# A decoder step on one core: the sampled sequences' keys turned on VectorE, and their attention interleaved with the prompt's out-projection

## The chip, the core and the metric

The kernel runs on one core of one Trainium2 chip. The core has TensorE (PE, with its weight loads PEld), VectorE (DVE), ScalarE (ACT), GpSimd (POOL) and SyncE (SP, which issues most transfers); 16 DMA engines move the data. The metric is device time in microseconds (us), lower is better.

## What is computed

One inference step of a decoder layer: 1,024 prompt tokens and 8 sampled sequences of 8 new tokens each, whose 1,024 past keys and values lie in a paged cache (8 pages of 128 keys for each sequence). The part that matters here, cut from the reference:

```python
def sample_attn(q, k, v, lam, k_past, v_past, rel_bias):     # 8 sequences, 8 heads, 2 maps a head
    s_past = diff_logits(q, q_pos, k_past, jnp.arange(past), rel_bias)
    s_new = diff_logits(q, q_pos, k, q_pos, rel_bias)
    w = diff_weights(jnp.concatenate([s_past, s_new], axis=-1), lam)
    return einsum('bhqk,bkhe->bqhe', w[..., :past], v_past) + einsum(..., w[..., past:], v)
...
x = x + jnp.einsum('btd,de->bte', g_a * y_a + g_b * y_b, lp['w_out'])       # out-projection
h2 = rms_norm(x, lp['norm_ffn'])
up = jnp.einsum('btd,df->btf', h2, lp['w_up'])                              # then the channel mixer
```

`diff_weights` is softmax of map 0 minus lam times softmax of map 1. All of it is float32. Where a product is not done in plain f32, each operand is split into a high part (rounded to fp32r) and a low part (the rest), and three products are summed: high by high, high by low, low by high.

## The kernel before

The program has four stages, each a block that all five engines enter and leave together: `front` (norm), `heads` (input projection, RG-LRU and prompt attention, one head after another), `sampled_and_out` (L1406 on) and `mixer`. At the end of a block every engine waits for all others, SP too. The change is in `sampled_and_out` and in the last transfers that SP issues in `heads`.

**A sampled sequence, before.** Each engine has the same loop over turns b = 0 to 8, 8 heads in each. For a head, TensorE turns the 1,024 keys (`turn_keys`, 8 transposes of 128x128 at L1735 into two banks `tb`), ScalarE copies a bank out as the high part (L1879), VectorE subtracts for the low part (L2045), and TensorE multiplies both parts with the queries (L1776, `qd`, 6 products of 344 columns). After the heads, VectorE sums and finds the maximum (L2012, L2090), ScalarE takes the exponent (L1921). The weights are turned by products with `C`, which holds the softmax's divisor and the signs (L1752, L1757), and are multiplied with the values (`page`, L1722: 32 columns of weights by 512 columns of values, into one of four strips of 32 partitions). A last step turns the result (`fold_heads`, L1710). Softmax and values of sequence b-1 lie in turn b. SP loads keys a sequence ahead into `k_raw` (two buffers of 8 pages) and values into `v_raw` (8 pages), a page being 512 KB; each page's number is first read from the page table (L1621).

**The out-projection, before.** After the last turn `out_tile(t)` (L1807) multiplies 128 merged tokens with `w_out`: 8 row blocks by 2 halves by 3 products, 48 products of 512 columns; there are 9 tiles, the last with 64 tokens. Tile 0 and 1 are begun in the last turn. Between tiles, `turn` (L1821) transposes the normed rows of the tile before, and `first_unit` (L1831) is the first unit of the mixer.

**What sets the order.** Every engine runs its list in program order and waits on semaphores. SP's list is one queue: a page load that waits for `page_done` holds all behind it.

Of the kernel before, what the change touches and what calls it, by code (L numbers as in the profile page):

```python
# [7 lines left out]
F32 = mybir.dt.float32  # L8
F32R = mybir.dt.float32r
# [381 lines left out]
def heads(nc, sb, sem, ins, outs, c):  # L391
# [206 lines left out]
    with nc.Block() as block:  # L598
# [19 lines left out]
        def _(sp):  # L618
# [9 lines left out]

            def load_pages(i):

                for n in (2 * i, 2 * i + 1):
                    page = sp.value_load(c.ptab[0:1, n:n + 1], min_val=0, max_val=ins["cache_k"].shape[1] - 1)
                    sp.dma_start(c.k0[:, c.k_first[n], :], ins["cache_k"][0, bass.ds(page, 1), :, :, :]
                                 .rearrange("a p h n -> p (a h n)")).then_inc(c.k_in[0][n // 4], 16)
# [7 lines left out]
            def body(f, first, last):  # L642
                m = 0
                for s in (TURN0 if first else TURN):
# [12 lines left out]
                    if s[0] == "P" and s[2] == 2:  # L657
                        g, ahead = W_NEXT[s[1]]
                        sp.wait_ge(ring_done, cur(f, NRING, RING[s]))
                        sp.sem_inc(settled, 1)  # L660
                        if last and ahead:
                            load_pages(done_last.index(s))
                        else:
                            load_w(f + ahead, g)
# [24 lines left out]
                    if s == ("QK", 7) and not last:  # L689
                        sp.wait_ge(c.tiles_out, 16 * 3)  # L690
# [34 lines left out]
            def load_sampled_bias():  # L725

                by_map = c.sbias_dram.rearrange("o (h m t) n -> m (o h) t n", h=H, m=2)
                for m in range(2):
                    sp.dma_start(by_map[m], bass.AP(tensor=c.bias_rows_dram.tensor, offset=DEC_T - 1,
                                                    ap=[[NU, H], [-1, DEC_T], [1, NKEYS]])).then_inc(c.tiles_out, 16)  # L730
# [505 lines left out]
        def _(pe):  # L1236
# [138 lines left out]
            pe.wait_ge(ttr_done, 16 * (H + 1))  # L1375
            for hf in range(2):
                pe.wait_ge(c.k_in[0][hf], 64)
                for n in range(4 * hf, 4 * hf + 4):
                    last_ = pe.transpose(ps[:, 3 + hf, 128 * (n % 4):128 * (n % 4 + 1)],
                                         c.k0[:, c.k_first[n], 0:128], c.ident[:, :])  # L1380
                last_.then_inc(c.tk0_done, 1)

SC = NKEYS // 3


def pair_select():

    row = np.arange(128)  # L1390
    head, m, t = row // 16, row // 8 % 2, row % 8
# [5 lines left out]
PV_EARLY = {}  # L1397
PV_AT = {4: (0, 1, 2, 3), 5: (), 6: (), 7: (), 8: (4, 5, 6, NPAGES)}
LAST = DEC_B - 1
OUT_SPLITS = [("m", 0), ("w", 0), ("w", 1), ("w", 2), ("w", 3), ("m", 1), ("w", 4), ("w", 5), ("w", 6), ("w", 7)]  # L1400
OUT_AT = {5: [("m", 0)], 6: [("w", 0)], 7: [("w", 1)], 8: [("w", 2), ("w", 3)]}
OUT_LOW = [x for x in OUT_SPLITS if x[0] == "m" or x[1] >= 4]
POOL_LOW = [x for h in range(H + 1) for x in OUT_AT.get(h, ()) if x not in OUT_LOW]


def sampled_and_out(nc, sb, sem, ins, outs, c):  # L1406
# [3 lines left out]
    S3 = ps[:, 0:3, 0:SC]  # L1410
    tb = [ps[:, 3, :], ps[:, 4, :]]
    pt = ps[:, 5, :]
    o2 = ps[:, 6, :]
    ptn = ps[:, 7, 0:NS]

    v_raw = sb("v_raw", [128, NPAGES, D], F32, 32768)
    vn_raw = sb("vn_raw", [128, D], F32, 65536)
    k_raw = [c.k0, sb("k1", [128, NPAGES, D], F32, 108544)]
    qd = sb("qd", [128, H * 128], F32R, 141312)
    slo = sb("slo", [128, NKEYS], F32, 145408)  # L1420
    sbias = sb("sbias", [128, NKEYS], F32, 150528)
    P = sb("P", [128, NKEYS], F32, 154656)
    pt_sb = sb("pt_sb", [128, NPAGES + 1, NS], F32, 158784)
    o2s = sb("o2s", [128, 512], F32, 163392)
    oT = sb("s_oT", [128, H, NS], F32, 167488)
    mg = sb("s_mg", [128, H, NS], F32, 169536)
    sel = sb("sel", [128, NS + 1], F32, 171584)
    p_new = sb("p_new", [128, 2, NS], F32, 176640)
    zeros = sb("s_zeros", [128, 2, DEC_T], F32, 177152)
    C = sb("C", [128, NS], F32, 172160)  # L1430
    sgn = sb("sgn", [128, 2], F32, 172416)
    mx = sb("s_mx", [128, 4], F32, 172448)
    eps = c.eps
    kt = sb("kt", [128, 2, 2, NKEYS], F32R, 178048)
    kt_hi, kt_lo = kt[:, 0, :, :], kt[:, 1, :, :]
    kn = sb("kn", [128, 2, H, NS], F32R, 206848)
    xn = sb("o_xn", [128, 2, D], F32, 202752)
# [8 lines left out]
    def strips(part, at):  # L1446

        q = qd[part, :]
        return bass.AP(tensor=q.tensor, offset=q.offset + at, ap=[q.ap[0], [144, HH], [1, DEC_T]])

    def q_hi_of(part, m, h0):

        return strips(part, 144 * h0 + DEC_T * m)

    def q_lo_of(part, m, h0):

        return strips(part, 144 * h0 + DEC_T * m + (NS if h0 < HH else -NS))

    def half_rows(s):

        lo = slice(NS, 128) if s == 0 else slice(0, NS)
        hi = slice(0, NS) if s == 0 else slice(NS, 128)
        return hi, lo
# [7 lines left out]
    v_in = [sem(f"v_in{n}") for n in range(NPAGES)]  # L1471
    vn_in = sem("vn_in")
    s_fill = sem("s_fill")
    tk_done = sem("tk_done")
    kthi_done = sem("kthi_done")
# [1361 lines left out]
```

## Time and profile before

| | us |
|---|---|
| median of 2 runs | 2019.01 (2018.39 to 2019.62) |
| the profiled execution's own time | 2017.05 |
| its span | 2015.2 |
| TensorE busy in it | 1967.5 |
| VectorE busy | 1312.9 |
| ScalarE busy | 937.4 |
| GpSimd busy | 37.0 |

The page gives one profiled execution. The span is cut into 40 slices of 50 us; GB/s says what the DMA engines moved in each. In a row of the timeline stand start, duration, engine, line, operation, output and inputs, shape and count; in square brackets, how long the engine stood idle before and for whom. A matmul's duration includes its way through the array, so the step from one start to the next tells what it costs.

### The profile page before, as it was taken

The numbers are of one execution on the slowest core, as the hardware profiler recorded it, in microseconds if no ns is written. First come the engines' busy times: TensorE is split into PE (matmuls) and PEld (weight loads), VectorE is DVE, ScalarE is ACT, GpSimd is POOL, SyncE is SP. The second block draws the span as 40 slices with busy tenths as digits, with TensorE's granted clock in tenths as the row PEclk, the third lists the DMA queues.
The fourth block names the chain that finished last, engine by engine and source line by source line (L and its number), as shares of the span: only waits on it lengthen the run. The fifth ranks groups of instructions, "written<-read, shape, count | busy, mean of one in ns | idle before, by whom it ended". The sixth has DMA issues, their size and how long they took to land. (4 is left out here: it accounts for less than half of the span.)

```text
span 2015.2 us, 35806 instructions
## 1 busy us (share of the span) xinstructions
PE 1967.5 (98%) x11872; PEld 1801.8 (89%) x11872; DVE 1312.9 (65%) x2891; ACT 937.4 (47%) x1705; POOL 37.0 (2%) x126
## 2 busy tenths in 40 slices
PE   6999999999999999899999999999999999999998
PEld 6999999999999999767768798999999998989896
DVE  6767667676676767666644485666657574748476
ACT  5766665657575757555554241322223131314033
POOL 0000000000000000000020000000000000000000
PEclk9999999999999999999999999999999999999999
DMA  6411111111111112599973121111111120202012
GB/s 197 150 58 54 58 53 57 53 57 53 57 53 57 53 55 76 199 349 338 342 278 110 35 81 32 55 42 53 42 44 52 32 63 22 73 22 73 5 50 100
DMA packets 167452, 183.25 MB, mean 91 GB/s; under 512 B 11045, under 2 KB 139589, under 8 KB 167349
## 3 DMA queue, kind: packets, MB, share of 16 engines
q1 hardware_dynamic: 166137, 181.24, 27.3%
q8 instruction: 43, 0.70, 0.1%
q10 hardware_dynamic: 1212, 0.81, 0.1%
q14 instruction: 60, 0.49, 0.1%
HBM read 162.82 MB, written 24.46 MB: 93 GB/s over the span
## 5 line engine op out<-in xcount | busy, mean ns | idle before, releaser
L1250 PE MATMUL ps<-h_hi,w_hi 128*128 128x384 f32 (+1 forms) x1152 | 387.0, 336 | 5.1 <-DVEq L967 3.4
L1250 PE MATMUL ps<-h_hi,w_lo 128*128 128x384 f32 (+1 forms) x1152 | 376.8, 327 | 0.0
L1250 PE MATMUL ps<-h_lo,w_hi 128*128 128x384 f32 (+1 forms) x1152 | 376.8, 327 | 0.0
L2410 PE MATMUL ps<-h_hi,f_w_hi 128*128 128x320 f32 (+1 forms) x1136 | 370.7, 326 | 0.8 <-PEq L1563 0.8
L2410 PE MATMUL ps<-h_hi,f_w_lo 128*128 128x320 f32 (+1 forms) x1136 | 370.4, 326 | 0.0
L2410 PE MATMUL ps<-h_lo,f_w_hi 128*128 128x320 f32 (+1 forms) x1136 | 370.2, 326 | 0.0
L2489 ACT ACTIVATE yc<-ps,f_prm 128x384 f32<-128x384 f32 x144 | 93.5, 654 | 555.7 <-PE ps L2410 382.8
L2390 PE MATMUL ps<-d_hi,act 128*128 128x512 f32 x816 | 257.0, 390 | 0.5 <-issue 0.5
L1250 PEld LDWEIGHTS ps<-h_hi,w_hi 128*128 128x128 f32 x1152 | 217.3, 189 | 9.0 <-issue 4.0
L1250 PEld LDWEIGHTS ps<-h_lo,w_hi 128*128 128x128 f32 x1152 | 217.4, 189 | 0.6
L1250 PEld LDWEIGHTS ps<-h_hi,w_lo 128*128 128x128 f32 x1152 | 217.0, 188 | 0.0
L2410 PEld LDWEIGHTS ps<-h_hi,f_w_hi 128*128 128x128 f32 x1136 | 213.2, 188 | 1.5 <-issue 1.1
L2410 PEld LDWEIGHTS ps<-h_lo,f_w_hi 128*128 128x128 f32 x1136 | 213.2, 188 | 0.3
L2410 PEld LDWEIGHTS ps<-h_hi,f_w_lo 128*128 128x128 f32 x1136 | 213.2, 188 | 0.0
L2544 DVE TENSOR_TENSOR x<-x,ps 128x512 f32<-128x512 f32 x144 | 97.8, 686 | 139.6 <-PE ps L2390 137.7
L2390 PEld LDWEIGHTS ps<-d_hi,act 128*128 128x128 f32 x816 | 153.2, 188 | 32.8 <-issue 0.7
L2390 PE MATMUL ps<-d_lo,act 128*128 128x512 f32 x432 | 168.2, 389 | 0.0
L2615 DVE SCALAR_TENSOR_TENSOR yc<-ps,f_prm,yc 128x383 f32<-128x383 f32 x144 | 82.2, 571 | 85.8 <-ACT yc L2489 82.3
L2045 DVE TENSOR_TENSOR kt<-ps,kt 128x512 fp32r<-128x512 f32 x128 | 82.7, 686 | 58.7 <-ACT kt L1879 58.3
L927 ACT ACTIVATE E<-E,nmx 128x256 f32<-128x256 f32 (+7 forms) x128 | 98.1, 768 | 14.3 <-DVE nmx L1195 9.8
L1191 DVE CUSTOM_DVE_ANT_0 E<-ps,bias 128x256 f32<-128x256 f32 (+7 forms) x128 | 91.4, 751 | 18.6 <-PE ps L1338 18.0
L1879 ACT ACTIVATE kt<-ps 128x512 fp32r<-128x512 f32 x128 | 72.1, 595 | 63.0 <-PE ps L1735 59.8
(301 smaller groups left out, 3181.0 us busy)
## 6 DMA issues: line engine op xcount, KB each, us to landing
k<-in_cache_k SPq DMA_DIRECT2D x64, 512.0 KB, 5.8
v_raw<-in_cache_v SPq DMA_DIRECT2D x64, 512.0 KB, 6.2
w_raw<-in_w_in SPq DMA_DIRECT2D x48, 512.0 KB, 4.0
f_raw<-in_w_up SPq DMA_DIRECT2D x48, 512.0 KB, 3.9
f_raw<-in_w_down SPq DMA_DIRECT2D x24, 512.0 KB, 3.5
bias<-bias_tiles_dram SPq DMA_DIRECT2D x8, 576.0 KB, 3.7
merged_dram<-mg SPq DMA_DIRECT2D x8, 544.0 KB, 2.7
ow_raw<-in_w_out SPq DMA_DIRECT2D x8, 512.0 KB, 7.5
```

Source lines behind the costliest of these rows:

```text
L927: act.activation(E[i][:, 0:n], E[i][:, 0:n], ACT.Exp, bias=nmx[:, i:i + 1], accum_out=den[:, i:i + 1]).then_inc(exp_done, 1)
L1191: dve.tensor_tensor_reduce(out=halves(E[i], j), in0=scores(i, j, first), in1=halves(bias, j, c0), scale=1.0, scalar=-3e38, op0=ALU.add, op ...
L1250: last_ = pe.matmul(bank(s)[:, 0:n], w[:, W_SLOT[g], k, :], x[:, k, off:off + n], start=(k == 0 and i == 0), stop=(k == KT - 1 and i == 2))
L1879: act.activation(kt_hi[:, h % 2, 512 * hf:512 * (hf + 1)], tb[hf], ACT.Copy)\
L2045: dve.tensor_tensor(kt_lo[:, h % 2, at], tb[hf], kt_hi[:, h % 2, at].bitcast(F32), ALU.subtract).then_inc(ktlo_done, 1)
L2390: l_ = pe.matmul(ps[:, down_bank(e), :], a, w[:, j, 512 * hf:512 * (hf + 1)], start=(j == 0 and i == 0), stop=(j == GF - 1 and i == len(pa ...
L2410: l_ = pe.matmul(ps[:, e % 6, 0:n], w[:, p, k, :], x[:, k, off:off + n], start=(k == 0 and i == 0), stop=(k == KT - 1 and i == 2))
L2489: act.activation(yc[:, e % 3, 0:n], ps[:, e % 6, 0:n], ACT.Identity, bias=prm[:, p, FCONV_W:FCONV_W + 1], scale=prm[:, p, FCONV_W - 1:FCON ...
L2544: dve.tensor_tensor(x2, x2, ps[:, down_bank(e), :], ALU.add).then_inc(add_done, 1)
L2615: link(dve.scalar_tensor_tensor(out=y[:, 1:np_], in0=x[:, 0:np_ - 1], scalar=w[1], in1=y[:, 1:np_], op0=ALU.mult, op1=ALU.add))
```

## The change

The diff is long; what it does, part by part:

- **Scores.** Keys are no longer turned on TensorE. VectorE transposes each page in place, 32x32 block by block (L1981 of the changed kernel, `STREAM_TRANSPOSE`, 8 a sequence). Scores are plain f32 products of 32 partitions by 32 columns of queries with 256 columns of keys (L1664, 128 a sequence), laid so that 16 consecutive ones lie at 16 different places of the array (4 groups of partitions `i`, 4 strips of outputs `h`), each group of partitions with a PSUM bank of its own. Splitting into high and low, its sums and the copies out fall away; the bias is added from PSUM (five operations instead of two sums and one).
- **Out-projection.** Tiles 0 to 6 go into the turns: step b of `sampled` does tile b-1 in five pieces (`fill`, 16+8+8+8+8 products) between scores, weights and values. Tiles 7 and 8 remain at the end. `w_out` is loaded and split at the stage's start. The low part of a tile is formed by GpSimd.
- **Values** have 4 page buffers instead of 8 (`vr`, `NV = 4`). Their loads stand ahead of the keys of two sequences later, each waiting for the buffer's `page_done`.
- **SP in `heads`.** Behind the last head's store of `merged_dram`, SP now loads 4 pages of keys and 4 of values, before the block ends. Four more key pages stand ahead of it.
- **Order.** Loops are unrolled, norms use Ln and Exp instead of Sqrt, and tiles are placed elsewhere in SBUF.

```diff
-                        for cc in range(3):
-                            keys = slice(SC * cc, SC * (cc + 1))
-                            for x, k in enumerate((kt_hi, kt_lo)):
-                                last = pe.matmul(S3[:, cc, :], qd[:, 128 * g:128 * (g + 1)], k[:, g % 2, keys],
-                                                 start=(g % HH == 0 and x == 0), stop=(g % HH == HH - 1 and x == 1))
...
+                for e in range(2):
+                    for j in range(NQ):
+                        for h in range(HH):
+                            J = NQ * (HH * e + h) + j
+                            for i in range(NQ):
+                                part = slice(32 * i, 32 * i + 32)
+                                pe.matmul(S[32 * h:32 * h + 32, i, :], qd[part, J, :],
+                                          keys[part, :, 32 * J:32 * J + 32],
+                                          start=(e == 0 and j == 0), stop=(e == 1 and j == NQ - 1))
...
+            for b in range(DEC_B):
+                t = b - 1
+                scores(b)
+                if b > 0:
+                    fill(t, 0)
+                    fold_heads(b - 1)
+                turn_weights(b)
+                if b > 0:
+                    fill(t, 1)
+                for run in range(4):
+                    values(b, run)
+                    if b > 0 and run < 3:
+                        fill(t, run + 2)
...
+                if b > 0:
+                    load_m(b)
+                    if b < LAST:
+                        load_x(b)
+                load_values(b, (4, 5))
+                load_values(b, (6, 7))
+                load_values(b + 1, (0, 1))
+                load_keys(b + 2, range(0, 4))
+                load_values(b + 1, (2, 3))
+                load_keys(b + 2, range(4, 8))
...
+                add_half(t - 1, 1)
+                turn_keys(b + 1, (0, 1))
+                softmax(b)
+                turn_keys(b + 1, (2,))
+                weights(b)
+                fold_rows(b - 1)
+                turn_keys(b + 1, (3, 4))
+                add_half(t, 0)
+                turn_keys(b + 1, (5, 6, 7))
...
+                        if last:
+                            load_next_keys(range(4, NPAGES))
+                            load_values()
```

**TensorE, first turn of the sampled stage.** Of the kernel before, two heads of sequence 0; `kt` holds the turned keys, `qd` the queries:

```order
L1703 UNCONDITIONAL_BRANCH [waits barrier_Pool_Activation_PE_DVE_SP_release]
L1735 MATMUL ps<-ident,k 128x128 [waits tk0_done,ktlo_done]
L1735 MATMUL ps<-ident,k 128x128 x3
L1735 MATMUL ps<-ident,k 128x128 [waits ktlo_done]
L1735 MATMUL ps<-ident,k 128x128 x3
L1776 MATMUL ps<-kt,qd 128x344 [waits ktn_done,ktlo_done,qdlo_done]
L1776 MATMUL ps<-kt,qd 128x344 x5
L1735 MATMUL ps<-ident,k 128x128 [waits ktlo_done]
```

Of the changed kernel, from the scores of sequence 1 on (`m_hi` and `w_hi` are a tile of the out-projection):

```order
L1664 MATMUL ps<-k,qd 32x256 [waits s_ttr_done,kt_done,qd_done]
L1664 MATMUL ps<-k,qd 32x256 x127
L1671 MATMUL ps<-k_new,qn 32x8 [waits ptc_done]
L1671 MATMUL ps<-k_new,qn 32x8 x7
L1739 MATMUL ps<-w_hi,m_hi 128x512 [waits ow_dlo_done,o_mplo_done]
...
L1712 MATMUL ps<-ident,o2s 128x128 [waits o2_done]
L1712 MATMUL ps<-ident,o2s 128x128 x3
L1682 MATMUL ps<-C,P 128x64 [waits ptc_done,c_done]
```

The transposes and their exchange with ScalarE and VectorE in every head are gone; one wait for all turned pages (`kt_done`) stands ahead of 128 score products, and out-projection products lie between them and the wait for the softmax (`c_done`).

**SP, end of `heads`.** Before, the store of the last head's merged rows is the last transfer of the block:

```order
L675 DMA out_v_rows_prompt<-rows 128x2x128 [waits row_done]
L678 DMA out_v_rows_sample<-rows 64x128
L697 DMA merged_dram<-mg 128x1088 [waits mg_done]
L598 UNCONDITIONAL_BRANCH [waits rows_out1,rows_out0,st_out]
L1616 UNCONDITIONAL_BRANCH [waits barrier_Pool_Activation_PE_DVE_SP_release]
```

Now eight page loads lie between the store and the block's end; the last of the keys and the last of the values:

```order
L631 TENSOR_LOAD ptab
L631 ISA x2
L632 ISA
L632 DMA k<-in_cache_k 128x1024
...
L632 DMA vr<-in_cache_v 128x1024
L598 UNCONDITIONAL_BRANCH [waits rows_out1,rows_out0,st_out]
L1578 UNCONDITIONAL_BRANCH [waits barrier_Pool_Activation_PE_DVE_SP_release]
```

So what SP issues there now stands ahead of the barrier for all engines.

## Rows read from the trace of the kernel before

**Rows 1.** The page: busy time and share of the engines; GB/s in 40 slices.
```profile
PE 1967.5 (98%) x11872; PEld 1801.8 (89%) x11872; DVE 1312.9 (65%) x2891; ACT 937.4 (47%) x1705; POOL 37.0 (2%) x126
GB/s 197 150 58 54 58 53 57 53 57 53 57 53 57 53 55 76 199 349 338 342 278 110 35 81 32 55 42 53 42 44 52 32 63 22 73 22 73 5 50 100
```

**Rows 2.** Windows: stretch, its length, busy of each engine, PE's clock, DMA share, GB/s.
```profile
833.00:840.00 7.00, 3.87 (x16) 3.15 (x15) 4.50 (x11) 3.59 (x9) 1.48 (x5) 0.52 0.57 207
885.00:1010.00 125.00, 120.86 (x864) 89.61 (x864) 77.66 (x152) 72.81 (x139) 9.62 (x50) 1.00 0.90 341
1050.00:1142.00 92.00, 91.34 (x431) 73.59 (x430) 40.57 (x51) 33.44 (x53) 0.00 (x0) 1.00 0.24 72
```

**Rows 3.** Timeline of TensorE, one turn of the sampled stage.
```profile
963.02 2.00 PE L1752 MATMUL ps<-C,P 128*128 128x64 f32 x16
...
965.05 1.19 PE L1776 MATMUL ps<-kt,qd 128*128 128x344 f32 x6
...
967.99 1.93 PE L1722 MATMUL ps<-v_raw,pt_sb 128*32 128x512 f32 x16
969.84 1.09 PE L1735 MATMUL ps<-ident,k 128*128 128x128 f32 x8
...
978.39 1.95 PE L1722 MATMUL ps<-v_raw,pt_sb 128*32 128x512 f32 x16
...
981.10 1.09 PE L1735 MATMUL ps<-ident,k 128*128 128x128 f32 x8
...
985.22 0.60 PE L1710 MATMUL ps<-ident,o2s 128*128 128x128 f32 x4
...
987.69 0.55 PE L1752 MATMUL ps<-C,P 128*128 128x64 f32 x3
```

**Rows 4.** Timeline of TensorE at the out-projection; 48 products of one tile lie between.
```profile
1060.14 1.02 PE L1844 MATMUL ps<-P,ones 128*128 128x512 f32 x2
1061.00 1.04 PE L1821 MATMUL ps<-ident,o_xn 128*128 128x128 f32 x8
...
1061.83 0.50 PE L1807 MATMUL ps<-ow_hi,m_hi 128*128 128x512 f32 x1
...
1072.87 1.04 PE L1821 MATMUL ps<-ident,o_xn 128*128 128x128 f32 x8
```

**Rows 5.** Timeline of TensorE in `heads`, two products of 64 partitions at once.
```profile
813.30 0.40 PE L1338 MATMUL ps<-k_lo,q_hi 64*128 64x512 f32 x2
813.54 0.39 PE L1338 MATMUL ps<-k_hi,q_lo 64*128 64x512 f32 x2
```

**Rows 6.** By shape: busy us, mean ns of one; idle before it.
```profile
L2103 DVE TENSOR_TENSOR m_lo<-o_raw,m_hi 128x1024 fp32r<-128x1024 f32 x6 | 7.3, 1219 | 2.6 <-ACT m_hi L1948 2.6
L1191 DVE CUSTOM_DVE_ANT_0 E<-ps,bias 128x256 f32<-128x256 f32 x16 | 6.1, 415 | 0.0
L1921 ACT ACTIVATE P<-P,s_mx 128x1032 f32<-128x1032 f32 x8 | 9.3, 1158 | 3.2 <-DVE s_mx L2093 3.0
L1597 POOL TENSOR_TENSOR ow_lo<-ow_raw,ow_hi 128x1024 fp32r<-128x1024 f32 x4 | 10.5, 2638 | 0.5 <-ACT ow_hi L1895 0.5
```

**Rows 7.** DMA in 885 to 1010 us: busy tenths and GB/s in 40 slices of 3.1 us.
```profile
DMA  9999993899999928999999399999983999999758
GB/s 337 375 402 414 406 408 136 279 333 396 384 409 414 405 102 298 273 393 414 414 406 408 80 315 376 358 409 419 408 350 94 287 376 418 413 408 404 295 159 266
```

**Rows 8.** The page's DMA issues: count, KB each, median us to landing.
```profile
f_raw<-in_w_down SPq DMA_DIRECT2D x24, 512.0 KB, 3.5
```

**Rows 9.** Timeline of SP's queue at the end of `heads`.
```profile
833.70 0.36 SPq L697 DMA_DIRECT2D merged_dram<-mg  x1
835.94 2.57 SPq L1625 DMA_DIRECT2D k<-in_cache_k  x3
```

**Rows 10.** Timeline of TensorE: end of `heads`, begin of the mixer.
```profile
830.44 0.70 PE L1370 MATMUL ps<-sq,ones 128*128 128x256 f32 x2 [0.75 <-ACT oT L947]
...
1155.61 0.38 PE L2410 MATMUL ps<-h_hi,f_w_hi 128*128 128x320 f32 x1 [0.80 <-PEq L1563]
```

More of the change, by code:

```diff
@@ L1396 @@
 HH = H // 2
-PV_EARLY = {}
-PV_AT = {4: (0, 1, 2, 3), 5: (), 6: (), 7: (), 8: (4, 5, 6, NPAGES)}
+NQ = 4
+NV = 4
 LAST = DEC_B - 1
[L1400 to L1403, printed above, removed]
+NIN = 7
+KS = (4, 5, 6, 7, 0, 1, 2, 3)
@@ L1444, in strip, with quarter @@
         return o2[32 * q:32 * q + 32, :]
[L1446 to L1463, printed above, removed]
+    def quarter(x, i):
+        return x[:, 0:PAST].rearrange("p (n i c) -> p i n c", n=NPAGES, i=NQ)[:, i]
     def own_rows(hf):
@@ new lines, in values, with fold_heads, products, weights_wait @@
+                    if n < NPAGES:
+                        last.then_inc(page_done, 1)
+            def fold_heads(b):
+                pe.wait_ge(o2_done, b + 1)
+                for g in range(HH):
+                    last = pe.transpose(o2[:, 128 * g:128 * (g + 1)], o2s[b][:, 128 * g:128 * (g + 1)], c.ident[:, :])
+                last.then_inc(ot_done, 1)
+            def products(k):
+                return ((m_hi, w_hi(k)), (m_hi, w_lo(k)), (m_lo, w_hi(k)))
+            def weights_wait(k):
+                if k in POOL_W:
+                    pe.wait_ge(wplo_done, POOL_W.index(k) + 1)
+                else:
+                    pe.wait_ge(wdlo_done, DVE_W.index(k) + 1)
@@ new lines, in fill @@
+            def fill(t, part):
+                for at in range(*FILL[part]):
+                    hf, x = divmod(at, HALF)
+                    k, i = KS[x // 3], x % 3
+                    if x == 0:
+                        if hf == 0:
+                            pe.wait_ge(mplo_done, t + 1)
+                        if t > 0 or hf > 0:
+                            pe.wait_ge(add_done, 2 * t + hf)
+                    if t == 0 and hf == 0 and i == 0:
+                        weights_wait(k)
+                    m, w = products(k)[i]
+                    last = pe.matmul(part_sum, m[:, k, :], w[:, 512 * hf:512 * (hf + 1)],
+                                     start=(x == 0), stop=(x == HALF - 1))
+                    if x == HALF - 1:
+                        last.then_inc(half_done, 1)
@@ new lines, in out_tile @@
+            def out_tile(t, ks):
+                n, at = rows_of(t), bank_of(t)
+                if ks[0] == KS[0]:
+                    pe.wait_ge(mdlo_done, t - NIN + 1)
+                for k in ks:
+                    for hf in range(2):
+                        for i, (m, w) in enumerate(products(k)):
+                            last = pe.matmul(ps[0:n, at + hf, :], m[:, k, 0:n], w[:, 512 * hf:512 * (hf + 1)],
+                                             start=(k == KS[0] and i == 0), stop=(k == KS[-1] and i == 2))
+                if ks[-1] == KS[-1]:
@@ new lines, in _ @@
+            turn_keys(0, c.k_first)
+            signs()
+            turn_keys(1, (0, 1, 2))
+            softmax(0)
+            turn_keys(1, (3,))
+            weights(0)
+            turn_keys(1, (4, 5, 6, 7))
+            for k in DVE_W:
+                weight_low(k)
+            for b in range(1, DEC_B):
+                t = b - 1
+                if b > 1:
+                    add_half(t - 1, 1)
[7 more added lines that the diff above has]
+                turn_keys(b + 1, (5, 6, 7))
```

992 lines of the change are left out of this document (440 added, 552 removed).

## The prediction

> **What bounds the kernel now.** I read the busy shares first: TensorE is busy 98% of the span, no other engine over 65% [rows 1]. So time is won only where TensorE does less or waits less. The slices say where else to look: GB/s is near 340 in five slices of 40 and low elsewhere [rows 1], which is the sampled stage. The window of it has TensorE busy 120.86 of 125 us, VectorE 77.66, and 341 GB/s [rows 2]: TensorE bounds it, and the transfers are not far behind. The windows of the out-projection show TensorE full and only 72 GB/s [rows 2]. The change lays the two over each other, and takes work from TensorE.
>
> A turn's length is the step between two equal places: L1752 starts at 963.02, values at 967.99 take 1.85 (to 969.84) and at 978.39 another 2.71 (to 981.10), the turned weights 2.03 (to 965.05), the fold 0.60 [rows 3]. The next turn's L1752 starts at 987.69 [rows 3]: 24.7 us a turn (its 16 pages of 512 KB, 8.39 MB, at 341 GB/s give 24.6 [rows 2]). Turning keys and scoring take what is left, 24.7 - 4.6 - 2.0 - 0.6 = 17.5 us. The stretch that the change touches goes from the end of `heads` (831.1) to the first mixer product at 1155.6 [rows 10], 324.5 us.
>
> **The price of the new scores (S).** A plain f32 product of 512 columns takes 0.86 us (1060.14 to 1061.00, two instructions [rows 4]), so one of 256 columns 0.43, and 128 of them one behind another 55 us. But the eight value products of a run, the same kind with 32 columns of weights in four strips, take 1.85 us for 6.9 [rows 3]: 3.7 at once. And two products of 64 partitions in different groups of partitions take one step of 0.24 us [rows 5], as one product of the out-projection does (11.04 / 48 = 0.23 [rows 4]). No row shows both splits together. If all 16 places work at once, S is 3.4 us; if eight (four strips by the two groups that rows show), 6.9; if only the four strips overlap, 13.8. I take 5, between the first two, since each split alone runs at full rate. The Trainium skill (TensorE: Matmul & The Clock Gate, Part 3: Packing small matmuls) reports 10.6 times for 16 such places; by that S would be 55 / 10.6 = 5.2, an estimate that no run here shows yet.
>
> **A step of the changed stage on TensorE.** Out-projection tile 11.0 [rows 4], values 4.6, weights 2.0, fold 0.6 [rows 3], S 5, new keys 0.3, some restarts 0.4: 23.9 us, out of which a whole out-projection tile comes nearly free: before it was 24.7 and 11.0 apart.
>
> **What it waits for.** Per step the transfers are 16 pages, a merged tile and an `x` tile, 18 x 0.524 = 9.44 MB. The slices reach 402 to 419 GB/s while pages queue, and 279 to 376 in those behind a pause [rows 7]. At 405 a page is 1.29 us and a step 23.3; the four value buffers add pauses: values 4 and 5 are asked for only when 0 and 1 are used up, 2.7 + 1.8 us before they are wanted, and an unqueued 512 KB lands 3.5 us after issue [rows 8], two of them with SP's 1.1 us a page 4.6. Walked through from the end of values 4 and 5 of the step before: 14 transfers (2 values, 4 keys, 2 values, 4 keys, tile, `x`) run from 1.5 to 19.6; values 0 and 1 are used up at 17.6, so the next pair moves from 19.6 to 22.2 and is seen some 1 us later, at 23.2; it is wanted at 17.6 + 4.5 = 22.1. That is 1.1 us late, and I add 0.4 for the slower rate behind a pause: 23.9 + 1.5 = 25.4 us for steps 2 to 5. Steps 6 and 7 load no keys: 24. The Trainium skill (DMA: Bandwidth & Descriptors, Specifications) gives some 358 GB/s of HBM for a core: by it a step is 26.4 us of transfers and the sum 5 us more. The rows with 402 to 419 GB/s speak against it as a ceiling.
>
> VectorE has per step 8 transposes, the five bias and maximum operations (415 ns for 256 columns [rows 6]) 2.4 with what follows, 1.4 of residual, 0.9 of small ones. A 128x1024 transpose is in no row. The two shapes differ by 804 ns for 768 columns [rows 6], so 1024 columns without any start cost are 1.07 us, my lower bound; the upper is twice 1219 ns, as if each block were first filled and then emptied. I take 1.22, the nearest row: 9.8 + 4.7 = 14.5 us, hidden under TensorE's 24; without that cover it would be all of it. Its pages 0 to 2 stand ahead of the softmax, and the chain from scores over maximum (2.4), exponent (1158 ns [rows 6]) and divisor (0.5) takes 4.2, against 4.2 of cover by `fill` 0 and the fold. GpSimd's low part takes 2.6 [rows 6] in the 5 us of the scores.
>
> **The start.** All engines wait for SP at the block's end. Before, its last transfer was issued at 833.70 and the next stage's at 835.94 [rows 9]. Three pages took 2.57 us including the last's own time, 1.1 a page [rows 9]. Eight behind the store, 9 us, and four ahead of it that hold it back by about 1: the stage begins at 844.4 instead of some 834.5 (after the store, before the first load), ten microseconds in which TensorE does nothing. Then sequence 0 has no cover: 8 transposes 9.8, scores on a slow clock (PE's clock was 0.52 in 833 to 840 after a pause [rows 2]; 7), three more transposes beside, softmax 2.4, exponent 1.3, divisor 0.6, weights 2 to 4, values with two waits of 4.6 each for pages 4 to 7: 36 us in sum, for 12 us of TensorE's work. Sequence 1 waits for keys of sequence 2, asked for at the end of values 4 and 5: 27 us.
>
> **The end.** After the last values, tiles 7 and 8 (22), nine turns (9 x 0.83 = 7.5 [rows 4]), fold and sum 1.6, the mixer's first unit 8.5, waits 2.4: 42 us.
>
> **Sum.** 844.4 + 36 + 27 + 4 x 25.4 + 2 x 24 + 42 = 1099.0, where it was 1155.6: 56.6 us less. Checked by work: 8 x (17.5 - 5.3) = 98 us of TensorE saved, some 32 idle added at the start, some 9 in the steps. The profiled execution's own time is 2017.05, 1.8 over its span; the median is 2.0 above that. 2019.0 - 56.6 = 1962. A difference of 2% (40 us, below 1978.6) is about what a measurement can tell here.
>
> **The rivals.**
> - *Only the four strips overlap* (S = 13.8): the value rows show four at once and no more [rows 3]. Start +9, sequence 1 +6, four steps at 32.7 +29, two +17: 61 us back, 2024, slower than before. From S = 13 on the gain is gone. Against it: groups of partitions do overlap [rows 5]. 6 in 100.
> - *TensorE's clock drops*: steps with pauses of 1 to 2 us and small products run at 0.5 as at 833 to 840 [rows 2]; 7 x 20 us more, about 2100. Against it: the clock is 1.00 over 885 to 1010 with pauses in it [rows 2]. 3 in 100.
> - *The DMA engines bound every step* at the 341 GB/s of the window instead of 405: 27.7 + 1 us, 1978. For it: 279 to 376 GB/s behind each pause [rows 7]. Against: those are the pauses' own. 12 in 100.
> - *The transposes take 2.4 us*: the start grows by 13, each step to 27.5 since three stand in the softmax's chain; 1990. The Trainium skill (Vector Engine (DVE) Microarchitecture Reference, 3.8) says that a transpose sustains one element a cycle and lane, which speaks against this. 8 in 100.
> - *Better than that*: S at 3.4, pairs of values on time, the start 8 us shorter: 1940. 11 in 100.
>
> **Chances.** My forecast's own case, 1948 to 1976, has 60 in 100. The range 1938 to 1988 leaves out the two slow rivals, half of the transposes' and a third of the better case: it holds some 83 in 100. Faster by over 2%: the forecast's case, the better one and half of the DMA one, 0.76; slower by over 2% is the clock and a bad form of the strips, 0.04; the rest 0.20.
>
> **What the profile will show.** S: the step from L1664's first start to L1671's, 4 to 7 us. Steps of 24 to 27 us between two equal rows of L1682. The stage's first operation at about 844. VectorE's `STREAM_TRANSPOSE` at 1.1 to 1.3 us. Waits of L1703 for `vr` below 2 us a step and 3 to 5 in sequence 0. A clock below 1 only in sequence 0. The first mixer product near 1099. I am wrong if S is over 10, if a transpose takes over 2 us, or if the waits for pages exceed 4 us a step.

## The result and the profile after

The changed kernel takes 2002.0 us (median of 2 runs, 2001.8 to 2002.2) against 2019.0: a ratio of 0.992, interval 0.991 to 0.994. It is faster by 0.8%, 17 us, where the forecast said 57 us. The profiled execution's span is 2000.0 us, 15 under that of before.

From the page of the changed kernel: busy time of the engines, the GB/s, VectorE's transposes, the queue that brings instructions, and the page loads with their median time to landing.

```profile
PE 1910.3 (96%) x13152; PEld 1726.6 (86%) x13152; DVE 1280.0 (64%) x2835; ACT 877.6 (44%) x1694; POOL 37.5 (2%) x68
...
GB/s 201 150 59 55 58 54 57 54 57 54 57 54 57 54 55 76 207 279 291 304 312 233 58 64 21 66 32 54 43 54 43 40 56 23 73 22 74 9 46 101
...
q8 instruction: 55, 0.90, 0.2%
...
L1981 DVE STREAM_TRANSPOSE k<-k 128x1024 f32<-128x1024 f32 x64 | 75.2, 1218 | 46.2 <-DMA k<-in_cache_k 34.8
...
k<-in_cache_k SPq DMA_DIRECT2D x64, 512.0 KB, 6.2
vr<-in_cache_v SPq DMA_DIRECT2D x64, 512.0 KB, 5.0
```

Against [rows 1], TensorE is busy 57 us less, in 1,280 matmul rows more, and is at 96% of the span in place of 98%. The forecast had 98 us of its work off. Half-rate stretches count as busy, so part of that is hidden in the 57; the rest, and why only 17 us of time came of it, is what the experiments are about. The slices that had 338 to 349 GB/s have 279 to 312.

Windows of three steps (scores to scores) and three short ones, behind the holes that are told of below; columns as in [rows 2]:

```profile
915.00:947.00 32.00, 28.06 (x402) 17.61 (x411) 13.28 (x26) 8.47 (x27) 2.97 (x4) 0.95 0.85 307
979.00:1008.00 29.00, 25.97 (x381) 16.13 (x376) 13.28 (x26) 8.07 (x27) 2.40 (x4) 1.00 0.87 323
1040.00:1070.00 30.00, 26.58 (x414) 16.35 (x411) 13.28 (x26) 13.25 (x39) 3.49 (x4) 1.00 0.97 346
954.30:957.80 3.50, 3.50 (x63) 2.13 (x63) 0.99 (x5) 0.96 (x4) 0.00 (x0) 0.51 1.02 417
986.20:989.70 3.50, 3.50 (x66) 2.48 (x36) 2.07 (x13) 2.05 (x9) 0.00 (x0) 1.00 1.04 419
1015.80:1022.60 6.80, 6.80 (x33) 4.87 (x31) 3.50 (x15) 5.30 (x18) 0.19 (x1) 0.50 1.04 403
```

Before, 125 us of this stage had 121 of TensorE at clock 1.00 [rows 2]. Now a step of 32 us has 28 of it, and the clock is 0.51 in a stretch of 3.5 us in the next. Such a stretch follows five of the seven holes of sequences 1 to 7, of 3.4 us each, and of 6.8 us behind that of sequence 5 (1015.8). It does not follow that of sequence 4 (986.2), nor that of 6, and the steps that begin with these (979, 1040) are 29 to 30 us.

The timeline of TensorE over one step, from the scores of sequence 3 (L1664) to those of sequence 4; the 48 products of the tile (L1739) and most values (L1703) are left out. An x212 counts matmuls, each with a weight load of its own; a burst of scores has 256 of them, two to a product of the program:

```profile
946.72 4.55 PE L1664 MATMUL ps<-k,qd 32*32 32x256 f32 x212
954.25 2.15 PE L1664 MATMUL ps<-k,qd 32*32 32x256 f32 x44 [2.98 <-issue]
956.34 0.40 PE L1671 MATMUL ps<-k_new,qn 128*32 128x8 f32 x16
...
961.42 1.90 PE L1682 MATMUL ps<-C,P 128*128 128x64 f32 x16
...
973.63 1.05 PE L1703 MATMUL ps<-vr,pt_sb 128*32 128x512 f32 x4 [1.09 <-DMA vr<-in_cache_v]
...
978.51 1.34 PE L1664 MATMUL ps<-k,qd 32*32 32x256 f32 x56
```

The scores do not take 5 us but 9.6, from 946.72 to 956.34. The rate is as forecast: 212 in 4.55 us are 5.5 us for all 256, ten to eleven times as fast as the 55 us of one behind another. But 44 of them wait behind a hole of 2.98 us that no semaphore ends ("issue": the profile sees nothing that the engine waits for). In the waits of 830 to 1180 us (total, times, longest):

```profile
PE ps L1664 <- issue: 22.1, 8, 3.3
...
PE ps L1703 <- DMA vr<-in_cache_v: 7.0, 9, 2.8
```

Eight such holes, one in each burst, 22.1 us. (A bracket counts from the end of the matmul before, so from start to start a hole costs some 0.35 us more than it says.) Before, PE had no row that ends in "issue" in this stretch. Values wait 7.0 us for pages in all.

The start, in the timelines of SyncE's queue, of VectorE, and the end, in that of TensorE:

```profile
831.86 0.79 SPq L713 DMA_DIRECT2D merged_dram<-mg  x1
833.47 4.67 SPq L632 DMA_DIRECT2D k<-in_cache_k  x4
838.90 3.60 SPq L632 DMA_DIRECT2D vr<-in_cache_v  x4
843.03 0.33 SPq L1614 DMA_DIRECT2D sbias<-sbias_dram  x1
```

```profile
843.08 3.50 DVE L1981 STREAM_TRANSPOSE k<-k 128x1024 f32<-128x1024 f32 x3 [11.36 <-PEq L598]
```

```profile
1140.40 0.38 PE L2379 MATMUL ps<-h_hi,f_w_hi 128*128 128x320 f32 x1 [0.81 <-PEq L1541]
```

The first mixer product stands at 1140.4, 15.2 us earlier than in [rows 10], and 41.4 later than the forecast's 1099.0.

### The profile page after: what moved, and what is told of

The parts are those of the page before. It is cut to its first block and busy times, and to the rows that moved or that the text cites. A ratio compares the mean times of both kernels' runs of the same rounds, so it can differ in the third digit from the quotient of the medians.

```text
span 2000.0 us, 37541 instructions
## 1 busy us (share of the span) xinstructions
PE 1910.3 (96%) x13152; PEld 1726.6 (86%) x13152; DVE 1280.0 (64%) x2835; ACT 877.6 (44%) x1694; POOL 37.5 (2%) x68
## 5 line engine op out<-in xcount | busy, mean ns | idle before, releaser
L1981 DVE STREAM_TRANSPOSE k<-k 128x1024 f32<-128x1024 f32 x64 | 75.2, 1218 | 46.2 <-DMA k<-in_cache_k 34.8
L2359 PEld LDWEIGHTS ps<-d_lo,act 128*128 128x128 f32 x432 | 81.1, 188 | 16.6
```

What stands on the lines that cost most here:

```text
L1981: dve.transpose(keys, keys).then_inc(kt_done, 1)
L2359: l_ = pe.matmul(ps[:, down_bank(e), :], a, w[:, j, 512 * hf:512 * (hf + 1)], start=(j == 0 and i == 0), stop=(j == GF - 1 and i == len(pa ...
```

## Experiments: what the hole is

**Sixteen tiny products ahead of the stage.**

```diff
+            for _ in range(16):
+                pe.matmul(part_sum[:, 0:8], c.ident[:, :], c.ones[:, 0:8], start=True, stop=True)
             for b in range(DEC_B):
                 t = b - 1
                 scores(b)
```

> 16 tiny products (8 columns of ones into the bank that the tile's halves use later) stand ahead of sequence 0's scores; nothing else is changed. In the changed kernel each burst of 256 score products has one hole of about 3.3 us, at product 147, 204, 208, 212, 216, 220, 224 and 228 of the eight bursts. Theory A, the engine waits there for its next block of instructions: the blocks' borders lie at fixed distances in the instruction stream, so 64 more instructions ahead move every hole some 32 products earlier (about 115, 172, 176, ...) and leave its length at about 3.3 us; the total stays within 2 us of the changed kernel's. Theory B, the hole belongs to a place in the scores (a row of the array, a bank, data that comes late): the holes stay at 147, 204, 208, ...

Sequence 3 on TensorE's timeline:

```profile
947.57 3.92 PE L1664 MATMUL ps<-k,qd 32*32 32x256 f32 x180
955.23 3.27 PE L1664 MATMUL ps<-k,qd 32*32 32x256 f32 x76 [3.73 <-issue]
```

The hole has moved from matmul 212 to 180, by 32 (the 16 products are 32 matmuls), and in the others of sequences 1 to 6 from 204 ... 224 to 172 ... 192. The total is 2000.3 us in one run. So the place is one in the instruction stream, not in the scores. A step has some 380 matmuls, and in its 31.8 us the queue q8 moves three packets of 16 KB: one to about 127 matmuls with their weight loads, which I call a block. Theory B falls. In the first burst the hole came one block later, at 243. There the tiny products had run from 843.8 on, while the scores still waited for keys, and q8 moved a packet at 847.4, 5.7 us ahead of the scores at 853.1; in the changed kernel q8's first packet of the stage starts at 856.9, when the scores have run since 852.4. So the block with the border at 115 had been asked for early enough.

**Half the key columns.**

```diff
-     pe.matmul(S[32 * h:32 * h + 32, i, :], qd[part, J, :], keys[part, :, 32 * J:32 * J + 32],
+     pe.matmul(S[32 * h:32 * h + 32, i, 0:128], qd[part, J, :], keys[part, 0:4, 32 * J:32 * J + 32],
```

> Scores with half of the keys left out: each score product streams 128 columns in place of 256, with the same count of products. Theory A, a burst is set by the issue of its 512 instructions at about 21 ns a product: 256 x 21 = 5.4 us of work stay, the hole stays at 3.3 us or grows by nothing, and the burst keeps its 7 to 9.5 us. Theory B, the array (16 products side by side, columns streamed) sets it: the work falls from 5.4 to about 2.7 us and the burst to 6 us or below. Total by A within 5 us of the changed kernel's, by B 20 us lower.

```profile
945.09 3.05 PE L1664 MATMUL ps<-k,qd 32*32 32x128 f32 x212
952.50 1.35 PE L1664 MATMUL ps<-k,qd 32*32 32x128 f32 x44 [4.37 <-issue]
```

Neither theory held whole. The 212 now take 3.05 us instead of 4.55, so a burst is not bound by issue at 21 ns as I had said: columns count, though half of them save only a third. But the 1.4 us come back in the hole, 4.37 in place of 2.98, and the total hardly moves (1997.9 in one run). That is how a fixed delay behaves: the faster the block before is used up, the longer the wait for the next.

**Thin pages.**

```diff
-     sp.dma_start(dst, pool[0, bass.ds(page, 1), :, :, :].rearrange("a p h n -> p (a h n)"))
+     sp.dma_start(dst[:, 0:256], pool[0, bass.ds(page, 1), :, 0:2, :].rearrange("a p h n -> p (a h n)"))
```

> The page loads that the sampled stage issues bring 256 of 1,024 columns; three quarters of their data are left out, all instructions are the same. If transfers set the step (9.44 MB, 24 to 27 us at 1.22 to 1.29 us a page), it falls to what TensorE needs; so: theory A, TensorE's stream (work plus the instruction hole) sets 29 to 31 us a step, and a step loses only the 1 to 2 us that values now wait for a page: total 1990 to 1998. Theory B, transfers set it: steps fall to 24 to 26 us, total 1960 to 1970.

```profile
933.57 4.55 PE L1664 MATMUL ps<-k,qd 32*32 32x256 f32 x212
939.26 1.32 PE L1664 MATMUL ps<-k,qd 32*32 32x256 f32 x44 [1.14 <-issue]
```

```profile
934.00:960.00 26.00, 24.86 (x376) 15.73 (x348) 13.28 (x26) 8.12 (x26) 2.28 (x4) 1.00 0.39 122
```

1964.6 us in one run, Theory B's number, but not by its mechanism. With transfers at 0.39 the hole has shrunk to 1.14 us on sequence 3 and to 0.3 to 0.8 on the others from 1 on, there the clock never falls, no value waits, and steps are 25.4 to 26.4 us with TensorE busy 24.9 of 26. Without what its hole costs from start to start (0.7 to 1.5 us) each of these steps is 24.9 us: that is the stream's own work. My Theory A had the hole as independent of traffic, and that was wrong. TensorE enters the block ahead of the hole 128 matmuls before it. From there to the start of the next packet on q8 it is 3.5 us in the changed kernel and 0.8 here; to the scores' going on 5.9 and 3.6 (medians over sequences 1 to 6).

**Full pages, but few in flight during the scores.**

```diff
             def load_keys(b, pages):
                 if b < DEC_B:
-                    sp.wait_ge(score_done, b - 1)
+                    sp.wait_ge(score_done, b)
```

> SyncE issues the page loads of the keys two sequences ahead only behind the scores of the next sequence, one burst later than in the changed kernel; the same pages are loaded in full, but few are in flight while a burst of scores runs. In the changed kernel the border before the one with the hole is crossed at 948.3, the block's transfer starts 3.6 us later, takes 1.0, and the scores go on 5.9 us after the border; with thin pages that was 0.8 us, 1.3 and 3.5, and the hole 1.0 in place of 3.3. Theory A, the block of instructions stands behind page packets in the DMA engines: the transfer starts within 1 us of the border, the scores go on 3.5 us behind it, and the hole is 0.7 to 1.5 us, with full pages. Theory B, the lead has to do with something else that the thin pages changed: hole 3 us. Theory C for the time: pages then come late, steps of 31 to 35 us, total 2000 to 2030.

TensorE on sequence 3, the window of its burst, and q8 (packets, MB, share of 16 engines) from 1.2 to 2.4 us behind the entry into the block at 959.7:

```profile
958.11 4.56 PE L1664 MATMUL ps<-k,qd 32*32 32x256 f32 x212
963.31 1.32 PE L1664 MATMUL ps<-k,qd 32*32 32x256 f32 x44 [0.65 <-issue]
```

```profile
958.10:964.60 6.50, 5.85 (x262) 3.89 (x262) 0.00 (x0) 0.60 (x1) 1.97 (x2) 1.00 0.06 25
```

```profile
q8 instruction: 1, 0.02, 4.8%
```

The transfers stand at 0.06 to 0.24 in the bursts of sequences 1 to 6, where the changed kernel has 0.95 to 1.00. The hole is 0.65 us on sequence 3 and 0.1 to 0.4 on the other five, the packet starts 0.6 to 1.3 us after the border, and the burst takes 5.7 to 6.5 us, with full pages. (On sequence 7 pages are in flight again, 0.54 in the burst: the hole is 1.54.) In the changed kernel, which enters the block at 948.3, the packet starts at 951.9; its window, 3.5 to 4.9 us behind the entry:

```profile
q8 instruction: 1, 0.02, 4.4%
```

So Theory A is shown: TensorE's instructions come in blocks that the profile counts on the same 16 DMA engines as the pages, and while pages queue there a block's packet starts some 3 us later; the packet itself takes no longer (0.9 to 1.1 us on sequences 1 to 6, and 0.9 to 1.3 with few pages). In theory C only the size was off: 2046 us in one run, since everything that was held back comes late (steps of 38 us).

The Trainium skill (Runtime: NRT & Kernel Launch, Instruction fetch mechanics) says that each engine's instructions are refilled in 16 KiB blocks of 256 through a DMA queue of its own, and that this is mostly hidden. The trace agrees on the blocks (0.90 MB in 55 packets), and on their being hidden where instructions are slow; for the densest 5 us of this kernel it does not hold.

## Experiments: what the hole costs

**Slow work between the halves of the scores.** The last run of values of a sequence (`values(b, 3)`) is moved into the next sequence's scores.

```diff
-                scores(b)
+                scores(b, (0, 1))
+                if b > 0:
+                    values(b - 1, 3)
+                scores(b, (2, 3))
...
-                for run in range(4):
+                for run in range(3):
```

> The last run of values of a sequence (pages 6 and 7 and the new values, 6 products, 1.9 us) stands between the two halves of the next sequence's scores in place of ahead of them; same products, same data. Theory A, the hole in the scores is a late block of instructions, because 256 dense instructions are used up in 2.7 us while a block is asked for some 5.9 us before it can be used: 1.9 us of slower products in the block shorten the hole by about 1.8 us in each of seven bursts, total 13 us lower than the changed kernel's, 1985 to 1995. Theory B, the hole has another cause (a place in the scores): it keeps 3.3 us, total within 3 us, or higher by two changes of shape a step (1 to 2 us in all).

```profile
941.66 2.76 PE L1666 MATMUL ps<-k,qd 32*32 32x256 f32 x128
...
946.20 2.03 PE L1666 MATMUL ps<-k,qd 32*32 32x256 f32 x84
950.27 1.76 PE L1666 MATMUL ps<-k,qd 32*32 32x256 f32 x44 [2.05 <-issue]
```

1987.6 us, ratio to before 0.985 (0.983 to 0.987), some 14 us less than the changed kernel, as expected. The row shows 2.05 us; sequences 1 to 6 have 0.4 to 2.1 and sequence 7 none. So the 1.9 us of values did not come off each hole alike, but off the seven together: 8.1 us in place of 19.4.

**And eight products of the tile beside it.** Each later piece of the tile moves one place forward, and on VectorE `add_half(t, 0)` stands right behind `weights(b)`.

```diff
-FILL = ((0, 16), (16, 24), (24, 32), (32, 40), (40, 48))
+FILL = ((0, 8), (8, 24), (24, 32), (32, 40), (40, 48))
...
                 if b > 0:
                     values(b - 1, 3)
+                if b > 1:
+                    fill(t, 0)
                 scores(b, (2, 3))
```

> As the kernel with the last run of values between the halves of the scores, and behind that run stand the first 8 products of the next tile's half as well (1.8 us; every later piece of the tile moves one place forward, no product is added or left out; VectorE adds the first half to x right behind the weights' scale). The block of instructions with the scores then lasts 2.7 + 1.9 + 1.9 = 6.5 us against a lead of 5.9 to 7. Theory A: the hole (1.4 to 2.4 us with the values alone) falls to 0 to 0.5, steps fall from 29 to 27, total 1987.6 - 6 x 1.8 = 1975 to 1981. Rival, transfers: a step's page packets take 26.5 us of 16 engines and stand idle 3 to 4 us while SyncE waits for page buffers: steps stay at 28.5 to 30, total 1984 to 1989.

The hole was gone from sequence 2 on, and nothing was gained: 1987.1 us. TensorE on sequence 3, and VectorE ahead of its softmax:

```profile
940.64 2.76 PE L1666 MATMUL ps<-k,qd 32*32 32x256 f32 x128
...
947.23 2.76 PE L1666 MATMUL ps<-k,qd 32*32 32x256 f32 x128
...
956.95 2.14 PE L1686 MATMUL ps<-C,P 128*128 128x64 f32 x16 [2.37 <-DVE C L2024]
```

```profile
950.87 2.37 DVE L1993 STREAM_TRANSPOSE k<-k 128x1024 f32<-128x1024 f32 x2 [12.05 <-DMA k<-in_cache_k]
953.16 0.38 DVE L2009 CUSTOM_DVE_ANT_1 P<-ps,sbias 128x256 f32<-128x256 f32 x1
```

The scores are done at 950.2, but VectorE's order has two key pages ahead of the softmax. It had waited 12.05 us for them, began to turn them at 950.87, and reached the maxima at 953.16, 2.9 us late. TensorE's 2.37 us wait for the divisor is that delay. Whether the transfers' rate or VectorE's order made that wait, the next run decides.

**The softmax first on VectorE.**

```diff
                 softmax(b)
-                turn_keys(b + 1, (2,))
                 weights(b)
+                add_half(t, 0)
                 fold_rows(b - 1)
-                turn_keys(b + 1, (3, 4))
-                add_half(t, 0)
-                turn_keys(b + 1, (5, 6, 7))
+                turn_keys(b + 1, range(NPAGES))
```

(`turn_keys(b + 1, (0, 1))` ahead of `softmax(b)` is gone too; `add_half` stood there already in the kernel before this.)

> As the kernel with values and 8 tile products between the halves of the scores (1987.1 us), but VectorE runs the softmax and the weights' scale of a sequence first and turns all eight pages of the next sequence's keys behind them, in place of two ahead and one between. In that kernel VectorE stood 12.1 us waiting for a key page ahead of the softmax, which began 2.9 us after its scores, and TensorE waited 2.4 us for the weights' scale (9.9 us over five steps). Theory A, the wait moved from the hole to this place only by VectorE's order: it goes, steps fall from 29 to 27, total 1976 to 1982, and the 3 to 4 us of idle transfers stay. Theory B, the transfers bound the step: the keys then are turned too late, the next scores wait for them, and the steps stay at 28.5 to 29.5, total 1984 to 1989.

```profile
912.00:1017.60 105.60, 103.90 (x1514) 63.88 (x1512) 51.89 (x104) 33.50 (x104) 11.36 (x13) 1.00 0.99 361
```

```profile
962.75 1.05 PE L1707 MATMUL ps<-vr,pt_sb 128*32 128x512 f32 x4 [0.35 <-DMA vr<-in_cache_v]
963.98 1.05 PE L1707 MATMUL ps<-vr,pt_sb 128*32 128x512 f32 x4 [0.18 <-DMA vr<-in_cache_v]
```

1977.1 us, ratio 0.980 (0.978 to 0.981): 10 us less, Theory A. The window is that of steps 2 to 5: 26.4 us each, TensorE busy in 26.0, the clock 1.00 and the transfers at 0.99, 361 GB/s. The busy time flatters the stream: added up from start to start its products are 24.9 us, as with thin pages, and the other 1.5 us of a step stand at the values of pages 4 and 5, which wait for their pages; the two rows are one such place. So once the hole is gone the late values are what is left of the waits, and the 16 engines are busy all the time. No run tells apart how much of it is the transfers' rate and how much the order of the loads. In one point Theory A was wrong: the idle time of the transfers went as well. They are asked for when TensorE and VectorE have used up pages, and both do so earlier.

## Experiments: transfers, cover and the barrier

**Two key pages ahead of the value loads**, once in the changed kernel as it was and once with the spread scores.

```diff
+                load_keys(b + 2, (0, 1))
                 load_values(b, (4, 5))
                 load_values(b, (6, 7))
                 load_values(b + 1, (0, 1))
-                load_keys(b + 2, range(0, 4))
+                load_keys(b + 2, (2, 3))
```

> The changed kernel with its scores in one burst as they were, and only the two key pages loaded ahead of the loads that wait for a values buffer. Theory A, the hole and the half clock behind it set the step, and transfers only through the 1 us for which values wait: total 1995 to 2002. Theory B, the engines' idle 3.5 us a step is what the step lacks: 1980 to 1990.

> As the kernel before, and two of the eight key pages of a sequence are loaded ahead of the first load that waits for a values buffer, so that the 16 engines have 2.6 us of packets in the 3.5 us in which they stood idle. If the transfers bound the step once the hole is gone: 1 to 2.6 us less a step, total 5 to 15 lower than the kernel before (1965 to 1975). If TensorE bounds it (25.7 us of work a step): within 3 us of it. Against it: values of pages 4 to 7 may land later and their products wait: up to 10 us more.

With the scores in one burst: 2002.2 us (0.990 to 0.994 of before), nothing gained; the holes are as long. With them spread: 1979.7 (0.980 to 0.983), 7 us less, in the span (5 to 15) that I had given to transfers as what bounds the step. The rows say otherwise.

```profile
937.00:964.00 27.00, 26.31 (x381) 15.98 (x380) 13.00 (x27) 8.37 (x26) 2.62 (x4) 1.00 0.97 350
992.00:1019.00 27.00, 26.15 (x402) 16.13 (x406) 13.23 (x26) 8.38 (x26) 2.91 (x5) 1.00 0.98 351
```

```profile
PE ps L1708 <- DMA vr<-in_cache_v: 5.0, 11, 1.0
...
DVE k L1994 <- DMA k<-in_cache_k: 0.7, 3, 0.3
```

Steps are 26.7 us with the transfers at 0.97 to 0.98, and VectorE waits 0.7 us for keys over five steps, where it had waited 12.05 in one. So the transfers did not set the changed kernel's step. The 7 us are those of the wait on VectorE, taken away from the other side: by earlier keys here, by its order in the run before.

**Without the tile.** All but the first and last product of each half are left out.

```diff
                     m, w = products(k)[i]
+                    if 0 < x < HALF - 1:
+                        continue
                     last = pe.matmul(part_sum, m[:, k, :], w[:, 512 * hf:512 * (hf + 1)],
```

> Of each half of the out-projection's tile only the first and the last product are left, 44 of 48 products of a step are left out, so that a step's floor without the tile shows. Worked out: 11 to 12 us of TensorE go. Theory A, TensorE's stream sets the changed kernel's step (31 us): the step becomes 31 - 12 = 19 by TensorE and is then caught by the transfers at 25 to 27 us; total 2002 - 7 x 4 to 7 x 6 = 1960 to 1975. Theory B, something that is not TensorE (turning of keys on VectorE, softmax, the new K and V) sets the step: it stays at 29 us or above, total over 1990.

```profile
962.24 3.68 PE L1682 MATMUL ps<-C,P 128*128 128x64 f32 x16 [3.19 <-DVE C L2014]
...
973.44 1.05 PE L1703 MATMUL ps<-vr,pt_sb 128*32 128x512 f32 x4 [1.77 <-DMA vr<-in_cache_v]
975.46 1.92 PE L1703 MATMUL ps<-vr,pt_sb 128*32 128x512 f32 x4 [0.96 <-DMA vr<-in_cache_v]
```

```profile
948.00:982.00 34.00, 24.76 (x365) 11.68 (x366) 13.18 (x26) 8.59 (x27) 2.94 (x5) 0.70 0.81 285
```

2009.6 us in one run, beside 2000.3 for the kernel with the sixteen tiny products on the same chip: slower, with 12 us less of products a step. My Theory A subtracted work where it had to follow waits. What the tile had covered is bare: 3.19 us for the divisor, 1.77 and 0.96 for values. And the clock is 0.70 over the step, so that the weights take 3.68 us instead of 1.90. Not one limit but a chain of waits, run through at half clock for much of the step, keeps it at 31 to 34 us; which share each has was not measured.

**The barrier.** The eight page loads behind the last head's store are issued at the sampled stage's start instead.

```diff
                         if last:
-                            load_next_keys(range(4, NPAGES))
-                            load_values()
...
             sp.dma_start(sel[:, :], ins["pair_select"]).then_inc(const_in, 16)
+            for n in range(4, NPAGES):
+                load(1, n, ins["cache_k"], c.k1[:, n, :], c.k_in[1][n // 2])
+            for n in range(NV):
+                load(0, n, ins["cache_v"], vr[:, n, :], c.v_in[n])
```

> The 8 page loads behind the last head's store (4 of keys, 4 of values) are issued at the start of the sampled stage, behind its two small constants, so that the barrier no longer stands behind them on SyncE. My theory (the barrier waits for SyncE, which is held by its loads: the last head's work ended at 829.1, the stage's first instructions stand at 843.1): the stage starts 7 to 9 us earlier and the total falls by 5 to 9 us. Rival: the loads are only moved behind and sequence 0's and 1's values and keys come that much later, total within 2 us.

> Both edits of the two kernels before, in one kernel. If they act at different places (the stage's start; each of seven steps), the gains add: 1985 to 1995 less 5 to 9, so 1978 to 1988 by my theories; by the rivals, 2000 or more.

```profile
846.89 5.05 PE L1665 MATMUL ps<-k,qd 32*32 32x256 f32 x147 [17.29 <-DVE k L1982]
...
881.87 2.53 PE L1665 MATMUL ps<-k,qd 32*32 32x256 f32 x114
```

The first scores stand at 846.9 instead of 852.4, 5.5 us earlier, those of sequence 1 at 881.9 instead of 883.8: 2.0. The total is 2000.9 (0.991 to 0.994), not told apart from the changed kernel's. With the values between the scores 1986.7, again no more than 1 us. Here the rival was right: the pages that were moved behind come later.

**All of them.** The kernel with spread scores and keys ahead, plus the barrier edit; and that with the softmax first.

> As the kernel with spread scores and two key pages loaded ahead (1979.7 us), and with the 8 page loads behind the barrier. On its own that edit moved the start 5.5 us and the total 1.1 us. If the transfers of the first two sequences bound their start: again 0 to 2 us lower, 1977 to 1980. If TensorE does: 4 to 6 us lower, 1974 to 1976.

> As the kernel before this, with VectorE's softmax first. Its keys come early enough, so no wait stands ahead of the softmax there: by Theory A within 2 us of the kernel before (the wait that the order would take away is not there), and by a rival, turning that no longer fills VectorE's pause for the exponential ends later and the next scores wait: up to 5 us more.

1975.3 us (ratio 0.978 to 0.980) and 1974.6 (0.978 to 0.981). The barrier edit brought 4.4 us here (the two intervals just touch), near the lower end of what I gave for a start bound by TensorE, and the order of VectorE nothing measurable more, as Theory A said. The first mixer product of the last one:

```profile
1111.54 0.38 PE L2390 MATMUL ps<-h_hi,f_w_hi 128*128 128x320 f32 x1 [0.81 <-PEq L1538]
```

## Why the forecast was wrong

The steps of the sum, in its own terms, against the changed kernel's trace:

| term | forecast | measured | off |
|---|---|---|---|
| stage begins | 844.4 | 843.1 | -1.3 |
| sequence 0 | 36 | 40.7 (843.1 to 883.8) | +4.7 |
| sequence 1 | 27 | 31.2 (to 915.0) | +4.2 |
| steps 2 to 5 | 4 x 25.4 | 125.5 (to 1040.5) | +23.9 |
| steps 6 and 7 | 2 x 24 | 59.2 (to 1099.7) | +11.2 |
| the end | 42 | 40.7 (to 1140.4) | -1.3 |

They sum to the 41.4 us of the first mixer product.

- **S, the price of the scores, was right, and the step that failed is the one that put it into the step as 5 us of time.** With the hole it is 8.6 to 9.6 us in steps 2 to 5. The array's work is 5.4 to 5.5 us, where the forecast had 5 and the Trainium skill's 10.6 times (TensorE: Matmul & The Clock Gate, Part 3) gave 5.2; the trace agrees with both. The profile's sign for S, "4 to 7 us from L1664's first start to L1671's", failed: it is 7.3 to 9.7. I priced 256 matmuls by the array alone and did not ask how they come to the engine. Every stretch of before was thinner: 16 matmuls in the 1.93 us of values, 0.12 us each [rows 3], one in 0.23 us in the out-projection [rows 4]. At some 20 ns each, no row of before stood near.
- **The rival "TensorE's clock drops" had 3 in 100, and it half came**: the clock is 0.50 for 3.4 or 6.8 us behind most holes. Over steps 2 to 5 the clock lost 1.5 us a step, where the rival had 20. The evidence against it, a full clock in 885 to 1010, had 4.1 us of pauses in five turns [rows 2]; now one pause is of 3.
- **The term 23.9 for TensorE's stream was 1 us too small** without any hole: 24.9, from start to start. A piece of 8 tile products takes 2.05 us instead of 1.84 (11.0 for 48 [rows 4]), the 16 of the first 3.83, the tile 12.0 for 11.0. S is 5.4 for 5, the values are 4.8 for 4.6; weights, fold and new keys are 2.6 for 2.9. I had given 0.4 for restarts; each piece of the tile costs 0.15 to 0.2 us over its share of 11.0, and a step has five.
- **The late values were right**: 1.5 us forecast, 1.8 a step as the mean of steps 2 to 5 from start to start (the brackets of the waits have 0.8 of it, 1.09 in the row at 973.63). So were the transposes (1.22 us against 1.218), the start behind the barrier and the end. Sequence 0 had a hole too, of 2.65 us.
- **So the step of 25.4** (steps 2 to 5 are 31.4 in the trace) is 24.9 of work at full clock, 3.2 of hole (12.6 us in four, 11.2 of them in the brackets), 1.5 of clock and 1.8 of late values, each from start to start. The hole with the clock behind it is 4.7 of the 6.0 us missed, the stream 1.0 and the values 0.3.
- **That the DMA engines bound each step** (12 in 100, at 1978) was not so in the changed kernel, whose steps 2 to 5 have them at 0.79 to 0.87, yet they made the hole. With the hole out they stand at 0.97 to 0.99 over a whole step, in the kernel with the softmax first at 361 GB/s where the forecast counted on 405, and the kernels lie at 1975 to 1980: there this rival is near. The forecast treated transfers only as bytes that must be there in time. That they hold up something else on the same engines is in none of its cases, so no rival gave 2002.

The range ended at 1988; with the hole taken out, two key pages loaded earlier, eight loads moved behind the barrier and the softmax first on VectorE the same change gives 1974.6. The remaining 12.5 us to the forecast's 1962 are those of the first mixer product too, 1111.5 against 1099.0. The start has no part in them: in that kernel the scores of sequence 2 begin at 906.7, where the forecast had 907.4. Steps 2 to 5 take 106.8 us in place of 101.6 (26.4 to 26.9 each), and from there to the mixer it is 98.0 in place of 90.

## What to carry to other kernels

Packing small products makes a stretch dense in instructions, and instructions are themselves transfers: where a block of 256 is used up in 2.6 us and page loads fill the DMA engines, the engine stands still. Put slower products (of another tile, or values) between dense bursts, rather than behind them, and look for waits marked "issue" at a drifting index. When a wait is removed and nothing is gained, read which engine's order the next one hangs on before blaming the transfers.

## What the runs showed of the hardware

- TensorE's instructions come in blocks of 256 (16 KB, one packet of q8, some 1 us). The packet starts 0.6 to 1.3 us after the block ahead of it is entered where the DMA engines are nearly idle, 3.2 to 3.7 us where pages queue; matmuls go on some 3.3 and 5.9 us after the entry.
- Sixteen places of the array at once run f32 products of 256 columns at 21 ns a matmul over a burst (4.55 us for 212), and 14 ns (3.05 us) with 128 columns.
- Behind holes of 1.9 to 3.3 us the granted clock fell to 0.50 (1.2 GHz) within 1.5 us in five cases of seven, for 3.4 us in four and 6.8 in one, and stayed at 1.00 in the two others (2.9 and 3.0 us); what sets them apart is open. With holes of 0.3 to 1.1 us (thin pages, sequences 1 to 7) it stayed at 1.00.
- VectorE turns 128x1024 f32 in 32x32 blocks in 1.22 us, in place.
- Leaving work out of an engine made the kernel slower (2009.6 against 2000.3, one run each): waits that the work had covered stood bare, and the clock was 0.70 over a step. How much of it is the clock's was not measured.
